# A 1-core transformer kernel: five entries of its step tables, one rotation and two norm sums moved

## The reference

```python
def mla_attention(q_nope, q_rope, k_nope, k_rope, v, ...):
    s = (jnp.einsum('bqhd,bkhd->bhqk', qn, k_nope)
         + jnp.einsum('bqhr,bkr->bhqk', qr, k_rope)).astype(jnp.float32) * scale
    p = jax.nn.softmax(jnp.where(mask, s, -jnp.inf), axis=-1)
    return jnp.einsum('bhqk,bkhd->bqhd', p.astype(v.dtype), v)

def mla_layer(h, ...):
    c_q = rms_norm(rms_norm(h, g_norm) @ w_dq, g_q)
    q = (c_q @ w_uq).reshape(B, L, MLA_HEADS, MLA_NOPE + MLA_ROPE)
    q_rope = rotary(q[..., MLA_NOPE:], pos, MLA_ROPE_THETA, MLA_ROPE)
    ...

def conv_ffn(h, g_norm, w_in, conv_w, conv_b, w_out):
    a, b = jnp.split(rms_norm(h, g_norm) @ w_in, 2, axis=-1)
    ...
```

## Time and profile before

| | before |
|---|---|
| median of 3 runs | 1265.07 us |
| profiled execution | 1265.07 us, span 1263.3 us |
| TensorE busy, matmuls | 1239.6 us (98%) |
| TensorE busy, weight loads | 1181.9 us (94%) |
| VectorE busy | 870.0 us (69%) |
| ScalarE busy | 684.0 us (54%) |
| GpSimd busy | 127.2 us (10%) |
| HBM | 160 GB/s over the span |

### The profile page before, as it was taken

How to read it: one execution, slowest core, us unless ns; L and a number is a source line. 1 busy time by engine, 2 the same in 40 slices (tenths; PEclk the granted TensorE clock), 3 DMA queues, 4 the chain that set the end, 5 groups by cost and what they waited for, 6 DMA issues and landing times.

```text
span 1263.3 us, 26315 instructions
## 1 busy us (share of the span) xinstructions
PE 1239.6 (98%) x10099; PEld 1181.9 (94%) x10099; DVE 870.0 (69%) x1690; ACT 684.0 (54%) x1329; POOL 127.2 (10%) x142
## 2 busy tenths in 40 slices
PE   7999999999999999999999999999999999999999
PEld 6888999999996789999998889999999889999998
DVE  5888677777766867777677867666565666766553
ACT  5666455545465646555446765555345765555432
POOL 0000300001300030000462003000120001100000
PEclk9999999999999999999999999999999999999999
DMA  7323355434542135554467334555454333555551
GB/s 315 134 101 115 120 173 189 171 131 171 199 152 92 68 103 198 185 181 148 169 221 263 102 133 167 189 180 199 181 186 153 117 130 115 191 176 191 196 175 64
DMA packets 31567, 203.46 MB, mean 161 GB/s; under 512 B 3616, under 2 KB 4640, under 8 KB 10864
## 3 DMA queue, kind: packets, MB, share of 16 engines
q1 hardware_dynamic: 30096, 197.83, 44.1%
q0 software_dynamic: 800, 3.21, 0.7%
q10 hardware_dynamic: 576, 1.11, 0.3%
HBM read 201.09 MB, written 1.05 MB: 160 GB/s over the span
## 4 chain that ended last, share of the span: by engine, by line
PE 83%; DVE 9%; ACT 5%; issue 2%; POOL 0%; DMA 0%; SPq 0%; ACTq 0%; DVEq 0%
PE ps L709 24%; PE ps L710 23%; PE ps L711 23%; DVE w_lo L1771 5%; ACT w_hi L1300 2%; PE ps L1110 1%; PE ps L1078 1%; PE ps L1095 1%; PE ps L802 1%; PE ps L1056 1%; PE ps L803 1%; PE ps L804 1%; DVE h L1833 1%; PE ps L923 1%; PE ps L927 1%
## 5 line engine op out<-in xcount | busy, mean ns | idle before, releaser
L1771 DVE TENSOR_TENSOR w_lo<-raw,w_hi 128x1024 fp32r<-128x1024 f32 (+2 forms) x394 | 465.6, 1214 | 133.4 <-ACT w_hi L1300 132.6
L1300 ACT ACTIVATE w_hi<-raw 128x1024 fp32r<-128x1024 f32 (+2 forms) x394 | 379.0, 1002 | 178.7 <-PE ps L711 174.8
L709 PE MATMUL ps<-x_hi,w_hi 128*128 128x256 f32 (+2 forms) x1384 | 400.3, 289 | 11.4 <-DVE w_lo L1771 10.6
L710 PE MATMUL ps<-x_lo,w_hi 128*128 128x256 f32 (+2 forms) x1384 | 393.3, 284 | 0.0
L711 PE MATMUL ps<-x_hi,w_lo 128*128 128x256 f32 (+2 forms) x1384 | 392.8, 284 | 0.0
L709 PEld LDWEIGHTS ps<-x_hi,w_hi 128*128 128x128 f32 x1384 | 261.7, 189 | 17.6 <-issue 12.5
L710 PEld LDWEIGHTS ps<-x_lo,w_hi 128*128 128x128 f32 x1384 | 261.5, 189 | 0.6
L711 PEld LDWEIGHTS ps<-x_hi,w_lo 128*128 128x128 f32 x1384 | 261.5, 189 | 0.0
L709 PE MATMUL ps<-X_x_hi,w_hi 128*128 128x256 f32 (+2 forms) x568 | 162.4, 286 | 1.9 <-DVE h L1833 1.3
L710 PE MATMUL ps<-X_x_lo,w_hi 128*128 128x256 f32 (+2 forms) x568 | 160.9, 283 | 0.0
L711 PE MATMUL ps<-X_x_hi,w_lo 128*128 128x256 f32 (+2 forms) x568 | 160.6, 283 | 0.0
(11 more groups left out here) (310 smaller groups left out, 1769.4 us busy)
## 6 DMA issues: line engine op xcount, KB each, us to landing
raw<-in_weights SPq DMA_DIRECT2D x160, 1024.0 KB, 4.8
raw<-in_weights SPq DMA_DIRECT2D x32, 704.0 KB, 4.1
raw<-in_weights SPq DMA_DIRECT2D x4, 832.0 KB, 4.5
E_bias<-in_even_bias POOLq DMA_DIRECT2D x4, 768.0 KB, 8.5
cst<-in_consts SPq DMA_DIRECT2D x1, 1144.0 KB, 6.6
h<-in_tokens ACTq DMA_DIRECT2D x4, 272.0 KB, 6.3
raw<-in_weights SPq DMA_DIRECT2D x2, 512.0 KB, 6.1
out<-h SPq DMA_DIRECT2D x8, 128.0 KB, 4.8
```

The lines of the kernel that those rows point to most:

```text
L709: pe.matmul(target, hi, xs[0], start=start, stop=False)
L710: pe.matmul(target, hi, xs[1], start=False, stop=False)
L1300: act.activation(w_hi[:, to + a:to + b], raw[:, fr + a:fr + b], ACT.Copy).then_inc(hi_made, 1)
L1771: dve.tensor_tensor(w_lo[:, to + a:to + b], raw[:, fr + a:fr + b], w_hi[:, to + a:to + b].bitcast(F32), ALU.subtract).then_inc(lo_made, 1)
```

## The change

Three things are done. `SUM_AT` puts the norm sum of `in0` and `in1` behind chunk 5 of the first slot, no longer behind chunk 7. In the tables of stage B pair 1 gets exponentials in step 15 (16 before), norm in 16 (17) and transposes in 17 (19); pair 3 gets transposes in 26 (27); the mixes of pairs 0, 1 and 5 come in steps 18, 19 and 32 (19, 21 and 33). And each r block is rotated in the step of its own block, r0 in step 7 with kr, behind that step's maxima, copies and mix outputs.

```diff
--- before.py
+++ after.py
@@ -91,7 +91,7 @@
 SCALED_BY = {"a_in": "a_attn", "in0": "ffn0", "b_in": "b_attn", "in1": "ffn1", "e_in": "mix0", "up0": "mlp0", "o_in": "mix1", "up1": "mlp1"}
 
 
-SUM_AT = {"in0": ("ffn0", 0, 7), "in1": ("ffn1", 0, 7),
+SUM_AT = {"in0": ("ffn0", 0, 5), "in1": ("ffn1", 0, 5),
           "up0": ("mlp0", 1, 7), "up1": ("mlp1", 1, 7)}
 
 
@@ -123,12 +123,12 @@
              "e_o": ((), (0, 1, 3, 4)), "f_o": ((), (0, 1, 3, 4))}
 
 SCORES_AT = {"A": (5, 7, 9, 13, 15, 17, 21, 23), "B": (12, 14, 21, 23, 26, 28, 31, 32), "E": (5, 7, 9, 10, 12, 14, 16, 17), "O": (7, 9, 11, 13, 15, 19, 21, 23)}
-TURN_AT = {"A": (7, 9, 11, 15, 17, 19, 23, 25), "B": (15, 19, 24, 27, 29, 31, 33, 35), "E": (7, 9, 11, 12, 14, 16, 18, 19), "O": (9, 11, 13, 15, 17, 21, 24, 25)}
-MIX_AT = {"A": (8, 10, 12, 16, 18, 20, 24, 26), "B": (19, 21, 27, 29, 32, 33, 35, 36), "E": (9, 11, 13, 14, 16, 18, 19, 20), "O": (11, 13, 15, 17, 19, 23, 25, 26)}
-
-EXP_AT = {"A": (6, 8, 10, 14, 16, 18, 22, 24), "B": (13, 16, 22, 24, 27, 29, 31, 32)}
-
-NORM_AT = {"A": (7, 9, 11, 15, 17, 19, 23, 25), "B": (14, 17, 22, 25, 28, 30, 32, 34)}
+TURN_AT = {"A": (7, 9, 11, 15, 17, 19, 23, 25), "B": (15, 17, 24, 26, 29, 31, 33, 35), "E": (7, 9, 11, 12, 14, 16, 18, 19), "O": (9, 11, 13, 15, 17, 21, 24, 25)}
+MIX_AT = {"A": (8, 10, 12, 16, 18, 20, 24, 26), "B": (18, 19, 27, 29, 32, 32, 35, 36), "E": (9, 11, 13, 14, 16, 18, 19, 20), "O": (11, 13, 15, 17, 19, 23, 25, 26)}
+
+EXP_AT = {"A": (6, 8, 10, 14, 16, 18, 22, 24), "B": (13, 15, 22, 24, 27, 29, 31, 32)}
+
+NORM_AT = {"A": (7, 9, 11, 15, 17, 19, 23, 25), "B": (14, 16, 22, 25, 28, 30, 32, 34)}
 
 PLACES = {"A": (3, 7, 11, 15, 19, 23, 27), "B": (3, 7, 11, 15, 19, 23, 27), "E": (7, 15, 21), "O": (7, 15, 21)}
 
@@ -1992,9 +1992,6 @@
                         rope(st, 5)
                     for n in pair_at(NORM_AT, a, s):
                         latent_norm(a, n)
-                    r = s - 2 if s < 12 else s
-                    if s <= a.last and st.seq[r][1] == "r":
-                        rope(st, r)
                     for n in pair_at(SCORES_AT, a, s):
                         latent_maxima(a, n)
                     for n in pair_at(TURN_AT, a, s):
@@ -2007,6 +2004,8 @@
                         dve.wait_ge(x_rounded, x.rounded + n + 1)
                         hi, lo = xpair(n, T)
                         dve.tensor_tensor(lo[:, 0:2 + SEQ], bank(7, 0, 2 + SEQ), hi[:, 0:2 + SEQ].bitcast(F32), ALU.subtract).then_inc(x_rest, 1)
+                    if s <= a.last and st.seq[s][1] == "r":
+                        rope(st, s)
 
                     if 2 <= s <= a.last + 1:
                         refill(st, s - 1)
```

## The result

The changed kernel takes 1276.16 us (median, 1274.17 to 1277.82) against 1264.99 for the kernel before: a ratio of 1.009, 95% interval 1.0072 to 1.0107. It is slower, as forecast, but by 11.2 us and not by 6.4, and it lies outside the range given. The profiled execution took 1276.32 us, its span is 1274.5.

What follows compares the result with a forecast made beforehand. The prediction took TensorE's instruction list to bound the kernel, changeable only through gaps between matmuls; six terms, 0.85 + 0.8 + 1.1 + 1.2 + 0.8 + 1.6 = 6.35, on 1265.07 gave 1271.4 us, range 1268.3 to 1273.2.

Steps and rivals of the forecast that it cites:

- The six gaps: TensorE idle 1.4 to 1.5 us at A and B, 1.0 at C, 2.4 at D, 0.9 at E, 1.7 at F.
- D: Pair 1's earlier exponentials, norm, transpose: TensorE waits 2.4 us before the transpose, replacing gaps of 1.0 and 0.2; cost 1.2.
- F: Mix of pair 5 right behind pair 4's: waits until VectorE empties bank 7, gap 1.75 us, cost 1.6.
- E: r2's rotation behind pair 3's maxima, pair 3's transpose a step earlier: gap 0.95 us before scores 4, cost 0.8.
- A: Norm sum in `in0` 12 matmuls earlier: TensorE waits some 1.4 us for GpSimd's last addition into `acc`; cost 0.85.
- B: The same earlier norm sum in `in1`, waiting for `acc`, ready at 475.99; cost 0.8 us.
- C: r0's rotation ahead of the store of k1, which frees bank 0: second v block starts later; cost 1.1 us.
- Rivals 1 to 3: Faster, 1263.6, 4 in 100; C and E hidden, 1269.5, 19 in 100; no difference, 1267, 8 in 100.
- the one on the clock: Idle TensorE can drop to 1.2 GHz; whether D's 2.4 us gap does so was left a question, with no term.
- steps of 0.23 as a sign of being wrong: Matmuls stepping 0.23 us after the 2.4 us gap before pair 1's transpose would show the prediction wrong.
- that rival itself: Clock falls after D, 21 steps at 0.10 us more, 2.1: 1273.5; also gaps growing through late weight splits; 9 in 100.

## Why the prediction was wrong

Its account of the waits was right. The six gaps are where it put them, within 0.2 us of its lengths and with its releasers; its terms add to 6.35, the measured ones to 6.7, and the changed kernel with its latent gaps filled takes 1271.43 against the forecast of 1271.4. That agreement is partly luck: the fillers at D and F are 0.2 to 0.3 us longer than the gaps, those at E leave 0.23 us idle, and the start and the untouched stretches are off by some tenths with both signs.

Term by term: A and B (0.85, 0.8) measured 0.9 and 0.9; A's own working, 159.0 less 158.10 less the refill of 0.1, gives 0.8. C (1.1) 1.1. D (1.2) 1.3 with C's rest. E (0.8) about 0.9; the gap is 1.14 against 0.95, since scores 2 to scores 4 took 12.54 us and not 12.35. F (1.6) 1.6; the medians of F alone with its gap filled give 1.4. Rivals 1 to 3 asked for gaps that close, and none did.

The step that failed is the one on the clock. The prediction took the time to be the length of TensorE's list, which the change can alter only through gaps, and its sum has no term for a list that runs slower. It gave a fall 9 in 100, as a rival, at one place, D, at a price of 2.1. Measured, TensorE was busy 4 us longer with the same list: the clock fell in all five runs of the changed kernel, in the profile behind E (a gap of 1.14) and F (1.79), and the two falls cost 4.7. Behind D's gap, where the prediction wanted steps of 0.23 as a sign of being wrong, this profile has steps of 0.13. The range too was drawn from less than one fall, though three gaps of over 1 us stood in one stage: it ends at 1273.2, below the 1273.5 of that rival itself. The lack of evidence was said openly (no row showed a gap between 1 and 9 us), and a price that no row bounds should have widened the range.

The Trainium skill, "TensorE: Matmul & The Clock Gate", Part 1, has an idle stretch lower the clock and work raise it again. The runs agree, with gaps of 1.14 us and more; nearly all of the cost comes after the gap, when TensorE works again.

What stays open is which gap sets off a fall in which run, and so why the profiled execution of the changed kernel has two. Gaps of 1.3 and 1.4 between dense matmuls set off none in eleven runs, one of 1.14 between scores and transposes did in two profiles, and D's 2.27 did in six of seven runs of one kernel and in none of five of another (D, with A and C, and E and F undone). Length and surroundings both fit some of this, and where the gap falls in time may have a part; no run here separates them.

## What to carry to other kernels

A gap on TensorE has two prices: its length, and what the clock costs behind it; here gaps of 1.8 us and more cost 1.7 to 3.4 us again in most runs (and one of 1.14 did in two profiles), so a wait that is met a little late is best met before, and if it can't be, useless matmuls into a free bank gave 2 to 4.7 us back. Moving a wait ahead of the point where its operand is ready paid at none of the six places; read how early the operand is there before moving the instruction. And idle time that an edit seems to create may only have been gathered: with E and F undone three gaps of 2.1 together stood in place of one of 1.14.

## What the runs showed of the hardware

The clock falls late, when TensorE is back at work or nearly so: 1.2 and 2 us behind the ends of the gaps in the changed kernel, and with the sum at chunk 3 some 0.6 us ahead of the gap's end (the steps turn from 0.23 to 0.13 at about 159.3, and the fall lasted 6 x 0.28 x 2 = 3.4). So it is paid nearly in full, in matmuls at 1.2 GHz: the two falls of the changed kernel last 10.2 us, half of which is 5.1, and cost 4.7.

TensorE's step also differs between executions at a granted clock of 1.00. The windows from 300 to 350 and from 500 to 550, both without a gap, of the kernel before:

```profile
300.00:350.00 50.00, 50.00 (x396) 50.00 (x396) 35.42 (x48) 23.18 (x36) 15.15 (x12) 1.00 0.55 195
...
500.00:550.00 50.00, 50.00 (x421) 50.00 (x420) 38.08 (x63) 28.01 (x45) 0.00 (x0) 1.00 0.53 189
```

and of the changed kernel:

```profile
300.00:350.00 50.00, 50.00 (x401) 50.00 (x401) 35.94 (x49) 23.18 (x36) 15.16 (x12) 1.00 0.54 195
...
500.00:550.00 50.00, 50.00 (x418) 50.00 (x418) 38.06 (x61) 27.43 (x45) 0.00 (x0) 1.00 0.50 187
```

It did 1.3% more matmuls in the first and 0.7% fewer in the second, as the -0.68 and +0.8 of the ledger have it. The second pair of windows lies some 10 us apart in the program; matmuls of 258 columns behind the sum of `in1`, taken by themselves, step 0.119 us before and 0.121 after. Runs of the kernel before, all at a clock of 1.000, spread over 2.9 us (1263.67 to 1266.58, on two chips); what decides the step is open.
